# GpSimd subtracts each weight chunk in two pieces of 512 columns: a float32 model block of 512 tokens on one core

## The reference

```python
h = rms_norm(x, g_pre_mix[l]) * (1 + sc_mix) + sh_mix
y = mixer(h, w_in[l], ...)             # mLSTM heads and a gated convolution of 31 taps
x = x + gt_mix * rms_norm(y, g_post_mix[l])
h = rms_norm(x, g_pre_mlp[l]) * (1 + sc_mlp) + sh_mlp
f = jnp.square(jax.nn.relu(h @ w_ff1[l])) @ w_ff2[l]
x = x + gt_mlp * rms_norm(f, g_post_mlp[l])
```

## Time and profile before

| | |
|---|---|
| three runs, us | 2275.9, 2276.02, 2280.16 (median 2276.02) |
| profiled execution, us | 2276.22 |
| its span, first to last instruction, us | 2274.4 |
| mean granted TensorE clock | 0.993 |
| busy, us: TensorE / VectorE / ScalarE / GpSimd | 2221.9 / 1248.2 / 985.0 / 1113.6 |
| low parts on GpSimd (line 950) | 349, 842.5 us busy |
| high parts on ScalarE (line 1076) | 349, 367.7 us busy |
| HBM read, MB | 236.84 |

### The profile page before, as it was taken

How to read it: one execution, slowest core, us unless ns; L and a number is a source line. 1 busy time by engine, 2 the same in 40 slices (tenths; PEclk the granted TensorE clock), 3 DMA queues, 4 the chain that set the end, 5 groups by cost and what they waited for, 6 DMA issues and landing times.

```text
span 2274.4 us, 28719 instructions
## 1 busy us (share of the span) xinstructions
PE 2221.9 (98%) x10450; PEld 1750.4 (77%) x10450; DVE 1248.2 (55%) x2077; ACT 985.0 (43%) x1614; POOL 1113.6 (49%) x596
## 2 busy tenths in 40 slices
PE   7999999999999999999999999999999999999998
PEld 5886667788888878766778888887767688888886
DVE  4989846863556599984464122147776653221222
ACT  3368543333133335775343223234666653331323
POOL 2688833544344648875364444363322244443442
PEclk9999999999999999999999999999999999999999
DMA  8432205354656323220222323332212123323232
GB/s 318 138 94 75 67 29 162 129 203 145 237 173 204 93 80 97 75 85 28 65 75 93 101 93 97 97 95 78 77 55 65 47 93 93 103 92 98 96 98 87
DMA packets 206662, 240.39 MB, mean 106 GB/s; under 512 B 9762, under 2 KB 172378, under 8 KB 206554
## 3 DMA queue, kind: packets, MB, share of 16 engines
q1 hardware_dynamic: 205990, 238.76, 33.0%
q10 hardware_dynamic: 564, 0.21, 0.0%
HBM read 236.84 MB, written 2.10 MB: 105 GB/s over the span
## 4 chain that ended last, share of the span: by engine, by line
PE 83%; DVE 7%; POOL 3%; ACT 3%; issue 2%; DMA 1%; ACTq 0%; DVEq 0%; POOLq 0%; SPq 0%
PE product L2507 25%; PE product L2509 25%; PE product L2508 25%; PE product L2880 1%; POOL ring_low L950 1%; PE side L2864 1%; PE side L3075 1%; POOL slot_f L981 1%; PE product L3110 1%; DVE side L1884 1%; PE side L3095 1%; POOL slot_f L1003 1%; DMA ring_f<-in_w_out 1%; ACT ring_high L1076 1%; DVE side L1672 1%
## 5 line engine op out<-in xcount | busy, mean ns | idle before, releaser
L950 POOL TENSOR_TENSOR ring_low<-ring_f,ring_high 128x1024 fp32r<-128x1024 f32 (+1 forms) x349 | 842.5, 2418 | 1045.6 <-ACT ring_high L1076 1045.0
L2507 PE MATMUL product<-slot_r,ring_high 128*128 128x512 f32 (+1 forms) x2536 | 1006.1, 397 | 14.0 <-POOL ring_low L950 6.0
L2509 PE MATMUL product<-slot_r,ring_high 128*128 128x512 f32 (+1 forms) x2536 | 989.2, 390 | 0.0
L2508 PE MATMUL product<-slot_r,ring_low 128*128 128x512 f32 (+1 forms) x2536 | 988.4, 390 | 0.0
L1076 ACT ACTIVATE ring_high<-ring_f 128x1024 fp32r<-128x1024 f32 (+1 forms) x349 | 367.7, 1056 | 707.4 <-DMA ring_f<-in_w_ff 329.9
L2507 PEld LDWEIGHTS product<-slot_r,ring_high 128*128 128x128 f32 (+1 forms) x2536 | 475.9, 188 | 143.7 <-issue 30.7
L2509 PEld LDWEIGHTS product<-slot_r,ring_high 128*128 128x128 f32 (+1 forms) x2536 | 475.9, 188 | 101.9
L2508 PEld LDWEIGHTS product<-slot_r,ring_low 128*128 128x128 f32 (+1 forms) x2536 | 476.3, 188 | 97.0 <-issue 1.4
L1884 DVE SCALAR_TENSOR_TENSOR side<-slot_f,cols,side 128x512 f32<-128x512 f32 x380 | 253.5, 749 | 0.6
L1842 DVE SCALAR_TENSOR_TENSOR va<-product,sqt 128x512 f32<-128x512 f32 x96 | 66.3, 692 | 333.3 <-ACT sqt L1154 332.0
L1862 DVE TENSOR_TENSOR slot_f<-product,slot_f 128x512 f32<-128x512 f32 x64 | 44.2, 690 | 175.1 <-PE product L2509 175.1
(11 more groups left out here) (324 smaller groups left out, 2077.2 us busy)
## 6 DMA issues: line engine op xcount, KB each, us to landing
ring_f<-in_w_ff SPq DMA_DIRECT2D x128, 512.0 KB, 3.8
slot_f<-in_w_ada SPq DMA_DIRECT2D x48, 1024.0 KB, 7.2
ring_f<-in_w_in SPq DMA_DIRECT2D x96, 512.0 KB, 3.9
ring_f<-in_w_out SPq DMA_DIRECT2D x40, 512.0 KB, 3.4
ring_f<-in_w_up SPq DMA_DIRECT2D x32, 512.0 KB, 3.7
ring_f<-in_w_down SPq DMA_DIRECT2D x32, 512.0 KB, 3.7
slot_f<-in_x SPq DMA_DIRECT2D x4, 512.0 KB, 5.2
ring_f<-in_w_v SPq DMA_DIRECT2D x4, 512.0 KB, 3.5
```

What stands on the lines that cost most here:

```text
L950: pool.tensor_tensor(whole(ring_low[:, s, :, :], n), whole(ring_f[:, s, :, :], n), whole(ring_high[:, s, :, :], n).bitcast(F32), ALU.subtr ...
L2507: pe.matmul(out_ap, high, rhs_high, start=start, stop=False)
L2508: pe.matmul(out_ap, low, rhs_high, start=False, stop=False)
L2509: return pe.matmul(out_ap, high, rhs_low, start=False, stop=stop)
```

## The change

`low_part` issues the subtraction of a chunk as pieces of T = 512 columns: two instructions for a chunk of 1024 columns, and one of 512 and one of 64 for the chunk of 576. The wait for the high part stands before the first piece, the signal to TensorE (`low_ready`) behind the last. What is computed is the same.

```diff
                 wait(pool, place, high_ready, plan.split(i))
-                pool.tensor_tensor(whole(ring_low[:, s, :, :], n), whole(ring_f[:, s, :, :], n),
-                                   whole(ring_high[:, s, :, :], n).bitcast(F32), ALU.subtract).then_inc(low_ready.sem, 1)
+                low, raw, high = (whole(r[:, s, :, :], n) for r in (ring_low, ring_f, ring_high))
+                pieces = (n + T - 1) // T
+                for k in range(pieces):
+                    at = slice(k * T, min((k + 1) * T, n))
+                    ins = pool.tensor_tensor(low[:, at], raw[:, at], high[:, at].bitcast(F32), ALU.subtract)
+                ins.then_inc(low_ready.sem, 1)
```

## The result

The changed kernel takes 2281.43 us in the median of 20 runs (2277.59 to 2286.2), the kernel before, run beside it, 2276.21 us (2274.14 to 2280.98): a ratio of 1.0021, 95% interval 1.0015 to 1.0028. It is 5.2 us slower in the medians and 4.9 in the means; the forecast was 2275.4 us, the range ended at 2280.0. The profiled execution took 2280.0 us, with a span of 2278.2. One execution of one experiment, e13_only_27, took 5725.16 us; it is left out of that kernel's mean, and without it its median would be 2276.16 us.

What follows compares the result with a forecast made beforehand. TensorE, with matmuls in flight for 98% of the span, was taken as the bound, so only its few gaps count. From 2276.22 us, gains of 3.25 and losses of 2.4 gave 2275.4 us; range 2272.0 to 2280.0.

Steps and rivals of the forecast that it cites:

- Cost of a split: On GpSimd, each split low part takes 0.15 us more; over 349 chunks about 50 us more work.
- (g): Two TensorE waits of 1.7 us on line 1019's score sums, each behind a low part: loss 0.15 each, 0.3 us.
- (d): Path from 222.36 us to TensorE's wait at 238.01, through three low parts: loss 0.45, twice (two layers) 0.9 us.
- (e): Second layer, 1016.76 to 1041.0 us: GpSimd's four low parts delay TensorE, which waits for it: loss 0.6 us.
- (f): At 1617.68 us TensorE waits for a low part; VectorE slips between its halves: loss 0.15 + 0.44 = 0.6 us.
- (b): From 1640 to 1664 us VectorE comes 2.2 us earlier, shortening TensorE's wait at 1663.84: gain 0.65 us.
- (c): VectorE's copy at 416.51 us ends 0.75 us earlier, shortening TensorE's wait at 422.22: gain 0.5 us.
- (a): At 188.20 us VectorE's copy comes 1.06 us sooner for TensorE: gain 1.05, repeated in second layer, together 2.1 us.
- R1: Rival: VectorE doesn't get in between the halves, so gains vanish: 2278.8 us, chance 0.15.
- R2: Rival: TensorE low-clock stretches appear or vanish, about 1.7 us each: 2273.7 or 2277.1, with two 2272.0 or 2278.8; chance 0.15.
- R3: Rival: VectorE holds the second half at all 13 exposed splits, 0.59 us each: 2280.7 us, chance 0.05.
- R4: Rival: (b) brings the whole 2.2 us, losses (d) are absorbed, a half-clock stretch goes: 2271.2 us, chance 0.05.

Runs made afterwards that it cites:

- e13_only_27: Kernel before with only the low part of chunk 27 split, in both layers: median 2276.4 us, ratio 1.0001 to before.
- e1_mixers: Kernel before with low parts split only in the first block's mixers (chunks 0 to 55 of both layers): median 2284.39 us, ratio 1.0031.
- e10_late_not_43: Kernel before with low parts of chunks 32 to 55 of both layers split, except chunk 43: median 2277.67 us, ratio 1.0007.
- e6_only_28: Kernel before with only the low part of chunk 28 split, in both layers: median 2276.09 us, ratio 0.9998.
- e9_only_43: Kernel before with only chunk 43 split, in both layers (the low part ahead of the score sums): median 2278.91 us, ratio 1.0008.
- e11_best: Kernel before with only chunk 28 of both layers and chunks 13 to 32 of the second block split: median 2275.72 us, ratio 1.0000.

## Why the prediction was wrong, step by step

- **Cost of a split, 0.15 us:** right. 0.14 us at (g), 0.11 in the fence on GpSimd above, 0.14 in the overlap at chunk 27. By the 58 us more that GpSimd is busy it is 0.17.
- **Losses (d), (e), (f), (g):** right. 0.39 to 0.43 twice for 0.45, 0.55 for 0.6, 0.57 for 0.6, 0.14 twice for 0.15. VectorE did slip between the halves at (f): its two operations take 3.34 us for 5.58. A small one was missed, 0.11 us more between 272 and 300 us of the first layer.
- **Gain (b):** 1.34 us for 0.65. The gap at 1663.84 gave 0.7, as counted; 0.4 came at 1659 us and 0.25 just behind the gap, where I had counted nothing. e1_mixers and e10_late_not_43 show the same 1.1 us by 1664 us with whole chunks (five others none), so part of it is chance.
- **Gain (c):** 0.81 us for 0.5, right in kind. The gap is closed in 7 of the 9 profiled kernels that split chunk 56 and in 1 of the 8 that don't.
- **Gain (a): the step that failed.** It says "The second layer repeats this (a gap of 1.10 us): together 2.1 us", and it takes the order of the two engines ahead of 182.89 us for fixed, while four more chunks just before it were split too. By e6_only_28 the 1.05 us is exact if nothing else moves. With the neighbours split the start of the place moves by 0.3 us against VectorE's, which turns the order round: no gain, and a loss of 2.2 us or, beside a stretch, 0.8. Even without that the gain was mis-sized, since the gap exists only where no half-clock stretch precedes it, in 8 of 18 places: 0.9 us.
- **R1** (VectorE doesn't get in between the halves, 2278.8 us): fell. Line 1838's maximum is 1597 ns for 1915 (not near 1.3 us, though), and VectorE gets in between at 1064 us in e9_only_43 (the halves take 3.02 us).
- **R2** (the clock): this is the second cause. It named the price and even two stretches, but as chance in either direction and at 0.15. By such a stretch it means one of low granted clock, 0.57 in the mean from 1542 to 1550 us, and its 1.7 us is an estimate: the same 0.57 stands over 426 to 430, 795 to 799 and 1184 to 1188 us of before (windows), and 4 x (1 - 0.57) = 1.7. In the changed kernel's trace the new stretches at 363 and 1076 us raise the lag by 1.65 and 1.70. The stretch is tied to a place, the wait on line 1019, which the prediction handles in (g) at 0.15 us each. Over both layers that term is 0.3 us for the path, as predicted, and 2.2 us (by the traces) to 3 us for the clock, which the sum put at nothing.
- **R3** (holds everywhere, 2280.7 us): near in time, wrong in mechanism. No hold was found at (d), (e) and (g) beyond the 0.15 us.
- **R4**: its part about (b) came true, nothing else of it.

Put right, the sum is -0.8 as forecast; +2.1 for (a) not gained; twice (8 x 2.2 + 10 x 0.8) / 18 = 1.4 for the turned order against the kernel before, +2.8; 2.4 to 3.3 for chunk 43 less the 0.3 already counted, +2.1 to +3.0; -0.7 for (b) and -0.3 for (c). That is +5.2 to +6.1 us, for +5.2 and +6.9 measured. It is an account after the fact, from the same traces, and each term is good to about 1 us. Open are the clock part of 1.4 us in e6_only_28 and e11_best, and why a stretch comes at 178 and 940 us in one execution and not in the next.

## What to carry to other kernels

Where instructions of two engines hold each other up, as VectorE's subtractions (1.78 us for 0.68) and GpSimd's additions (1.83 us for 1.29) do here, the order between them can hang on a tenth of a microsecond: before counting a gain at one place, work out how much everything upstream shifts that place, and how far the order is from turning. A longer standstill of TensorE ahead of a dense stage may cost more in clock than in waiting (0.47 us more of waiting, and 1.7 us for the stretch behind it in 9 of 14 places), so an edit that makes the work in front of such a wait faster can lose time. To find a difference, compare when the same instruction starts in both traces, and in several executions, before taking a gap for a fixed property of the kernel.

## What was not expected of the hardware

- A TensorE wait of 2.2 us was followed by a stretch of some 3.4 us at a granted clock of 0.50 in 9 of 14 places, one of 1.7 us at the same point in 0 of 20. Each stretch cost 1.7 us there. At 1670 us it was 5 of 6 after 2.2 us and 0 of 11 after 1.75. At 178 and 940 us, after waits of 2.7 us, such a stretch comes in 19 of 34 places, in some executions and not in others.
- Two losses can cover each other: the stretch at 940 us and the gap of 1.1 us at 949 us didn't occur together in any of 18 places.
- Where VectorE's next subtraction and GpSimd's next addition both start before the subtraction that VectorE is at has ended, VectorE's went first in all 24 places in which the addition started at most 0.01 us ahead of it, and the addition took 1.77 to 1.85 us. GpSimd's went first in all 10 in which the addition started 0.14 to 0.17 us ahead: it took 1.35 to 1.39 us, and a subtraction of 0.68 us took 1.78. So the two don't run side by side there, and little time decides which goes first.
